# Cached-page work of the decode samples issued two tile-steps earlier in a hybrid S5/MLA step

## The reference, cut to what matters

```python
def mla_sample_attn(q_abs, q_pe, c_new, kpe_new, c_pool, kpe_pool, page_table, w_uv):
    c_past = c_pool[page_table].reshape(dbs, -1, KV_LORA)        # 8 x 2048 x 512
    kpe_past = kpe_pool[page_table].reshape(dbs, -1, QK_ROPE)    # 8 x 2048 x 64
    s_past = (einsum('bqhr,bkr->bhqk', q_abs, c_past) + einsum('bqhe,bke->bhqk', q_pe, kpe_past)) * SOFTMAX_SCALE
    w = softmax(concatenate([s_past, s_new], -1))
    o_lat = einsum('bhqk,bkr->bqhr', w[..., :n_past], c_past) + einsum('bhqk,bkr->bqhr', w[..., n_past:], c_new)
    return einsum('bqhr,rhv->bqhv', o_lat, w_uv)

def mla_prompt_attn(...):   # 8 heads, causal, 528 keys
    o = softmax(where(kpos <= qpos, scores, -inf)) @ c, then w_uv
```

## Time and profile before

| what | us |
|---|---|
| median of 3 runs | 1088.49 (1087.4 to 1095.65) |
| the profiled execution's own time | 1086.38 |
| its span | 1084.5 |
| V stage ends (first `scores` of head 0) | 682.85 |
| attention loop and tail, to the output projection's first product | 682.85 to 874.11 |

### The profile page before, as it was taken

How to read it: one execution, slowest core, us unless ns; L and a number is a source line. 1 busy time by engine, 2 the same in 40 slices (tenths; PEclk the granted TensorE clock), 3 DMA queues, 4 the chain that set the end, 5 groups by cost and what they waited for, 6 DMA issues and landing times.

```text
span 1084.5 us, 26976 instructions
## 1 busy us (share of the span) xinstructions
PE 1026.1 (95%) x10657; PEld 942.7 (87%) x10657; DVE 626.0 (58%) x1341; ACT 381.1 (35%) x805; POOL 157.5 (15%) x257
## 2 busy tenths in 40 slices
PE   5999999999999999999999999788988899999996
PEld 5999999999999999989899987565655569999996
DVE  4685445542676656587785545687888542322333
ACT  6621122222233221145642331544554323322333
POOL 0002310000320000011422412323343100000000
PEclk9999999999999999999999999799999899999999
DMA  9548743322363434165455766858998685233214
GB/s 261 120 135 146 171 109 98 98 72 77 112 166 108 135 98 116 50 156 181 148 154 152 232 197 206 271 185 269 280 297 267 211 272 169 77 104 89 77 39 158
DMA packets 202061, 169.81 MB, mean 157 GB/s; under 512 B 37579, under 2 KB 166086, under 8 KB 200646
## 3 DMA queue, kind: packets, MB, share of 16 engines
q1 hardware_dynamic: 178854, 119.12, 39.4%
q0 software_dynamic: 11616, 29.06, 9.0%
q10 hardware_dynamic: 11496, 20.32, 5.3%
HBM read 140.84 MB, written 25.26 MB: 153 GB/s over the span
## 4 chain that ended last, share of the span: by engine, by line
PE 81%; DVE 6%; ACT 5%; issue 3%; DMA 3%; SPq 0%; POOL 0%; ACTq 0%; DVEq 0%
PE gemm L2156 14%; PE gemm L2157 14%; PE gemm L2158 14%; PE gemm L2525 5%; PE gemm L2527 5%; PE gemm L2526 5%; PE misc L2429 3%; PE gemm L2444 2%; PE gemm L2474 2%; PE misc L2243 1%; PE misc L2196 1%; PE misc L2233 1%; DMA toep<-kall 1%; PE misc L2408 1%; PE gemm L2332 1%
## 5 line engine op out<-in xcount | busy, mean ns | idle before, releaser
L2156 PE MATMUL gemm<-xh,w_hi 128*128 128x260 f32 (+2 forms) x1056 | 302.0, 286 | 0.1
L2157 PE MATMUL gemm<-xl,w_hi 128*128 128x260 f32 (+2 forms) x1056 | 299.9, 284 | 0.0
L2158 PE MATMUL gemm<-xh,w_lo 128*128 128x260 f32 (+2 forms) x1056 | 299.4, 284 | 0.0
L2156 PEld LDWEIGHTS gemm<-xh,w_hi 128*128 128x128 f32 x1056 | 198.7, 188 | 2.6 <-issue 1.9
L874 ACT ACTIVATE w_hi<-w_raw 128x2048 fp32r<-128x2048 f32 (+3 forms) x63 | 90.7, 1440 | 312.6 <-PE gemm L2158 278.8
L2158 PEld LDWEIGHTS gemm<-xh,w_lo 128*128 128x128 f32 x1056 | 199.1, 189 | 0.0
L2157 PEld LDWEIGHTS gemm<-xl,w_hi 128*128 128x128 f32 x1056 | 199.0, 188 | 0.0
L1336 DVE TENSOR_TENSOR w_lo<-w_raw,w_hi 128x2048 fp32r<-128x2048 f32 (+3 forms) x63 | 110.8, 1759 | 152.1 <-ACT w_hi L874 150.1
L2525 PE MATMUL gemm<-comb_hi,w_hi 128*128 128x260 f32 x448 | 128.5, 287 | 1.2 <-DVE comb_lo L2013 1.1
L2527 PE MATMUL gemm<-comb_hi,w_lo 128*128 128x260 f32 x448 | 126.7, 283 | 0.0
L2526 PE MATMUL gemm<-comb_lo,w_hi 128*128 128x260 f32 x448 | 126.6, 283 | 0.0
(11 more groups left out here) (416 smaller groups left out, 2058.2 us busy)
## 6 DMA issues: line engine op xcount, KB each, us to landing
w_raw<-w_in SPq DMA_DIRECT2D x35, 1024.0 KB, 6.3
ckv<-cache_ckv POOLq DMA_DIRECT2D x76, 256.0 KB, 3.9
w_raw<-w_out SPq DMA_DIRECT2D x16, 1024.0 KB, 5.8
ckv<-cache_ckv SPq DMA_DIRECT2D x52, 256.0 KB, 3.7
z_d<-ev ACTq DMA_DIRECT2D x16, 260.0 KB, 2.0
w_raw<-w_glu SPq DMA_DIRECT2D x8, 512.0 KB, 4.1
yt<-x_prompt SPq DMA_DIRECT2D x4, 1024.0 KB
w_raw<-w_uq SPq DMA_DIRECT2D x8, 384.0 KB, 3.6
```

The lines of the kernel that those rows point to most:

```text
L2156: pe.matmul(acc, a, xa, start=k == 0, stop=False)
L2157: pe.matmul(acc, a, xb, start=False, stop=False)
L2158: last = pe.matmul(acc, b, xa, start=False, stop=k == k_tiles - 1)
```

## The change

`LEAD = 2`: all page work of the samples stands two steps earlier against the prompt's tiles.

- Groups 0 and 1 are turned by VectorE in the V stage (v = 5 and 6) into a buffer of their own, `ct_first`, on dead weight memory; the first pair is scored by TensorE in the V stage at v == 8, ahead of that tile's transposes. To free the scores' bank `gemm[2]` the V tiles take turns on three banks (`V_BANK`). ScalarE's spreading into `rep` moves from v == 6 to v == 5, and `build_query(0)` from behind the stage to v == 6. SP, ScalarE and VectorE each wait once for that first pair (`sc_ready` 1) before memory of `ct_first` is written again.
- In the loop pair p is scored in step 2p - 1 instead of 2p + 1, and group n + 3 is turned in step n.
- Sample s has its maximum and exponential in step 4s + 2; VectorE's `turn_sample_weights` stands ahead of that step's page transposes. Its weights are spread at the top of step 4s + 3, ahead of that step's `scores`, and copied by ScalarE behind that step's `exponential`. Its groups are summed in steps 4s + 4 (two, between `turn_last_weights` and `weigh_values`), 4s + 5 and 4s + 6.
- `copy_o`, `build_query`, the samples' stores and the reloads move along. The last sample's groups are summed two in step 31, one behind `turn_last_weights`, one behind the last `weigh_values`.
- Slots 3, 4 and 5 of the ring change places, SP loads group 5 instead of 3, and `cnew` has another address.

```diff
-            return 4 * (i // 4) + 4 + ((0, 2, 3, 4) if i // 4 < N_SAMPLE - 2 else (0, 2, 2, 2))[i % 4]
+            return min(4 * (i // 4) + 4 - LEAD + ((2, 2, 3, 4) if i // 4 < N_SAMPLE - 1 else (1, 1, 2, 2))[i % 4], N_TILES)
...
-        BY_SYNC = 3
+        BY_SYNC, LEAD = 5, 2
...
@@ SP
+            sp.wait_ge(sc_ready, 1)
             for h in range(2):
                 load_v(h)
...
@@ ScalarE, loop
                 scale_rows(n)
-                if n % 4 == 0 and n >= 8:
-                    copy_o(n // 4 - 2)
+                s = (n + LEAD) // 4 - 1 if (n + LEAD) % 4 == 0 else -1
                 if n % 4 == 0 and n:
                     copy_last_turned(n - 1)
-                    sample_exp(n // 4 - 1)
+                if s >= 0:
+                    sample_exp(s)
                 if n + 1 < N_TILES:
                     exponential(n + 1)
-                if n % 4 == 0 and n:
-                    sample_weights(n // 4 - 1)
-                    if n // 4 + 1 < N_HEADS:
-                        head_hi(n // 4 + 1)
+                if s >= 1:
+                    copy_o(s - 1)
+                if n % 4 == 0 and n and n // 4 + 1 < N_HEADS:
+                    head_hi(n // 4 + 1)
+                if n % 4 == 3:
+                    sample_weights(n // 4)
                 copy_turned(n)
...
@@ VectorE, V stage
+                if v in (5, 6):
+                    turn_pages(v - 5, 0, 2)
+                    turn_pages(v - 5, 2, 4)
+                    turn_rotary(v - 5)
...
@@ VectorE, loop
-                if n % 4 == 0 and n:
-                    sample_max(n // 4 - 1)
+                group = n + 1 + LEAD
+                if (n + LEAD) % 4 == 0:
+                    sample_max((n + LEAD) // 4 - 1)
...
                     maximum(n + 1)
-                    turn_pages(n + 1, 0, 2)
-                if n % 4 == 0 and n:
-                    turn_sample_weights(n // 4 - 1)
+                if (n + LEAD) % 4 == 0:
+                    turn_sample_weights((n + LEAD) // 4 - 1)
+                if group < N_GROUPS_OF_PAGES:
+                    turn_pages(group, 0, 2)
                 if n + 1 < N_TILES:
                     normalise(n + 1)
-                    turn_pages(n + 1, 2, 4)
-                    turn_rotary(n + 1)
+                if group < N_GROUPS_OF_PAGES:
+                    turn_pages(group, 2, 4)
+                    turn_rotary(group)
...
@@ TensorE, V stage
+                    if v == 8:
+                        page_scores(0, 0, 16)
...
@@ TensorE, loop
             for n in range(N_TILES):
+                if n % 4 == 3:
+                    spread_page_weights(n // 4)
                 if n + 1 < N_TILES:
                     scores(n + 1)
+                if n % 4 == 0 and n:
+                    turn_last_weights(n - 1)
                 for i in range(N_GROUPS_OF_PAGES - 4):
-                    if freed_at(i) == n and i % 4:
+                    if freed_at(i) == n:
                         weigh_pages(i // 4, i % 4)
                 if n % 4 == 0 and n:
-                    turn_last_weights(n - 1)
                     weigh_values(n // 4 - 1)
-                    spread_page_weights(n // 4 - 1)
-                if n % 2:
-                    page_scores(n // 2, 0, 6)
+                pair = (n + LEAD) // 2 if n % 2 else N_PAIRS
+                if pair < N_PAIRS:
+                    page_scores(pair, 0, 6)
                 turn_weights(n)
-                for i in range(0, N_GROUPS_OF_PAGES - 4, 4):
-                    if freed_at(i) == n:
-                        weigh_pages(i // 4, 0)
+                if n == N_TILES - 1:
+                    for c in range(2):
+                        weigh_pages(N_SAMPLE - 1, c)
...
             turn_last_weights(N_TILES - 1)
+            weigh_pages(N_SAMPLE - 1, 2)
             weigh_values(N_HEADS - 1)
-            spread_page_weights(N_SAMPLE - 1)
-            for c in range(4):
-                weigh_pages(N_SAMPLE - 1, c)
+            weigh_pages(N_SAMPLE - 1, 3)
```

More of the change, by code:

```diff
@@ L1081, in head_hi, with build_query @@
                 act.activation(hh[h % 2][:], hraw[:], ACT.Copy).then_inc(head_hi_done, 1)
+            def build_query(s):
+                if s >= 2:
+                    act.wait_ge(sc_ready, 2 * s - 2)
+                for a in range(4):
+                    rows, cols = slice(32 * a, 32 * a + 32), slice(a * N_HEADS, (a + 1) * N_HEADS)
+                    act.activation(qx[rows, s % 2, :, cols], rep[rows, 0:16, :, s], ACT.Copy)
+                    last = act.activation(qxr[rows, s % 2, :, cols], rep[rows, 16:18, :, s], ACT.Copy)
+                last.then_inc(query_built, 1)
             for v in range(10):
@@ L1794, in head_lo, with turn_pages, turn_rotary @@
                 tt(hh[u][low, rot_cols], hraw[low, rot_cols], hh[u][low, rot_cols].bitcast(F32), ALU.subtract).then_inc(head_lo_done, 1)
+            def turn_pages(n, first, last):
+                by_sync = (1 if first == 0 else 0) if n >= RING else (1 if n == BY_SYNC else 0)
+                dve.wait_ge(page_loaded[by_sync][n % RING], loaded_counts(n)[by_sync])
+                if first == 0 and n >= 3:
+                    dve.wait_ge(sc_ready, (n - 3) // 2 + 1)
+                out = ct_first[:, n, first:last] if n < 2 else ct[:, n % 3, first:last]
+                dve.transpose(out=out.rearrange("p x r -> p (x r)"),
+                              in_=ckv[n % RING][:, first:last].rearrange("p x r -> p (x r)"))
+            def turn_rotary(n):
+                dve.transpose(out=kt[:, n % 3].rearrange("p x e -> p (x e)"), in_=kpe[n % RING][:].rearrange("p x e -> p (x e)")
+                              ).then_inc(page_turned, 1)
             dve.wait_ge(rope_loaded, 64)
@@ L1903, in _ @@
             maximum(0)
+            dve.wait_ge(sc_ready, 1)
             dve.wait_ge(c_t_ready, 6)
@@ L2347, in scores, with page_scores @@
                 last.then_inc(scores_ready, 1)
+            def page_scores(pair, first, last):
+                s, half = divmod(pair, 2)
+                if first == 0:
+                    pe.wait_ge(page_turned, 2 * pair + 2)
+                if first == 0 and half == 0:
+                    pe.wait_ge(query_built, s + 1)
+                    if s >= 2:
+                        pe.wait_ge(sexp_done, s - 1)
+                buffers = buffers_of(pair)
+                c0 = (s % 2) * P + half * 64
+                for r in range(first, last):
+                    for j in range(4):
+                        pe.matmul(SC[32 * j:32 * j + 32, c0:c0 + 64].rearrange("p (g t) -> p g t", g=2), qx[:, s % 2, r, :],
+                                  turned(pair)[:, buffers, j, r * 32:(r + 1) * 32], start=r == 0, stop=False)
+                if last < 16:
+                    return
+                for e in range(2):
+                    for j in range(4):
+                        last = pe.matmul(SC[32 * j:32 * j + 32, c0:c0 + 64].rearrange("p (g t) -> p g t", g=2), qxr[:, s % 2, e, :],
+                                         kt[:, buffers, j, e * 32:(e + 1) * 32], start=False, stop=e == 1)
+                last.then_inc(sc_ready, 1)
             pe.wait_ge(gemm_read, B_V + 2)
@@ L2430, in weigh_values @@
                 last.then_inc(pv_done, 1)
-            def page_scores(pair, first, last):
-                s, half = divmod(pair, 2)
-                if first == 0:
-                    pe.wait_ge(page_turned, 2 * pair + 2)
-                if first == 0 and half == 0:
-                    pe.wait_ge(query_built, s + 1)
-                    if s >= 2:
-                        pe.wait_ge(sexp_done, s - 1)
-                buffers = buffers_of(pair)
-                c0 = (s % 2) * P + half * 64
-                for r in range(first, last):
-                    for j in range(4):
-                        pe.matmul(SC[32 * j:32 * j + 32, c0:c0 + 64].rearrange("p (g t) -> p g t", g=2), qx[:, s % 2, r, :],
-                                  ct[:, buffers, j, r * 32:(r + 1) * 32], start=r == 0, stop=False)
-                if last < 16:
-                    return
-                for e in range(2):
-                    for j in range(4):
-                        last = pe.matmul(SC[32 * j:32 * j + 32, c0:c0 + 64].rearrange("p (g t) -> p g t", g=2), qxr[:, s % 2, e, :],
-                                         kt[:, buffers, j, e * 32:(e + 1) * 32], start=False, stop=e == 1)
-                last.then_inc(sc_ready, 1)
             def spread_page_weights(s):
```

86 lines of the change are left out of this document (32 added, 54 removed).

## The result

The changed kernel takes 1099.24 us (median of 7 runs, 1095.45 to 1104.62), the kernel before 1090.61 us in the same comparison: a ratio of 1.0105, 95% interval 1.0073 to 1.0137. The forecast was 1087, no change; the result is slower by about 1%, inside the range and outside the likeliest case. The profiled execution took 1099.02 us, its span is 1097.3 us, 12.8 more than that of the profiled execution before.

A forecast was written before the change was run, and what follows sets the result against it. A closed chain of waits between TensorE and VectorE, 20.2 us a head, was taken as the bound. 0 + 1.2 + 3.9 - 3.4 - 2.7 = -1.0 gave 1085.4, forecast 1087 by the median, range 1071 to 1104.

The forecast's parts named there:

- the term of the six heads: Steps 4 to 27: 0.65 us more a head, with the old order's stalls kept at their sum; +3.9 us.
- late pages: Rival: pages of group 4s + 8 land 1 us late a head, 1094 us; chance 0.10, shared with unchanged `head_hi`.
- The clean head: A head of the attention loop without stalls: -1.36 + 0.3 + 1.73 = +0.67, to 20.85 us.
- (a): Spreading moves to step 4s + 3, so `head_hi` follows `exponential` and `head_lo` no longer waits: -1.36 us a head.
- (b): Two sums ahead of the weighted values hide TensorE's 0.71 us round trip but add 1.04: +0.3 us a head.
- The gate waits: VectorE, behind its pages of a head's first step, waits 1.5 us or more at the gate in each head.
- (c): Sample's maximum moves to a head's third step, into VectorE's chain, with the weights' transpose: +1.73 us, bounds 0 and 1.73.
- The clock rival: Rival: 2.1 us of TensorE idling in step 4s + 3 drops its clock; 2.7 us a head, 1106; chance 0.20.
- V stage and head 0: Up to step 4: the first pair's 2.4 us hidden, 0; head 0's new sample maximum less some slack, +1.2.
- step 0's wait for ScalarE: At head 0, step 0 waits 3.79 us for ScalarE, so TensorE's scores coming 2.4 us later cost 0.
- Step 28 and the tail: Last head's first step 12.26 to 8.9 us, -3.4; tail to the output projection 26.96 to 24.3 us, -2.7.

The follow-up runs named there:

- the even version: Changed kernel with a sample's first group summed in step 4s + 3 instead of in 4s + 4 beside the second: 1087.34 us, ratio 1.0001.
- the filled version without reloads: Changed kernel without the page ring's reloads, with 14 dummy products in TensorE's three gaps of step 4s + 3: 1089.61 us, ratio 1.0013.

## Why the prediction was wrong

**The step that failed** is the cost at nothing of the reloads in the term of the six heads: +3.9 us were forecast and +15.5 measured. Without reloads the two orders differ by 7.2 there; the reloads add 12.8 to the changed order and 4.6 to the old one. The prediction priced late pages only as a rival, with 1 us a head and a chance of 0.10, at the group whose slot is freed first (4s + 8). That group came in time; the third one did not, by up to 5.5 us. The working counted one slot's issue and landing at the landing times of the earlier trace rows, which were those of an evenly fed queue. It did not ask what the DMA engines do meanwhile. In five heads of the changed kernel, 715 to 835 us, the two largest queues move 30.6 MB, 6.1 a head; at the 297 GB/s that the even version reaches in its stretch without idling that is an estimate of some 20.6 us, a whole head, which leaves no room to make up for idle time of these engines. The change makes them idle 3 to 4 us a head: the samples' pages are wanted two steps earlier, but the first sum of a sample, which frees a slot, stays in step 4s + 4, now beside the second. The head is then the transfer plus the idling, 23.6 to 24.6 us by these numbers; 23.41 was measured, and by the packets 3.6 of it are idle and 19.8 are not. The Trainium skill ("Trainium Kernel Development and Optimization", "Key Constraints") has all queues on the same 16 engines; the runs agree so far as GpSimd's pages land in 3.1 us and not 4.9 when SyncE's are not loaded.

That this is the cause is shown by the even sums, with all the bytes and one sum a step earlier: 1087.3 us, 11 to 12 less. Without reloads and with half of them the changed order takes 1086.3 to 1086.6. That all three lie at the forecast of 1087 is luck. The forecast kept the old order's stalls, and without reloads, where these are gone, the change still costs 10.8 us and not -1: the first pair on TensorE, two falls of the clock, a stall and a longer clean head. With even sums that loss is balanced by the old order's 11 us of stalls, of which the changed order keeps less (3.0 us of issue stalls, 7.2 before).

**The clean head** was forecast at 20.85 and is 20.49, but not by the steps of the prediction. (a) The wait for `head_hi` was worth 0.1 and not 1.36: VectorE's chain closed no sooner than TensorE's own work, 18.5 us and its gaps. The prediction took one closed chain for the bound where a second lay 0.1 us behind it; its joint at 791.07 was a coincidence, as the earlier trace rows show no idle time of TensorE ahead of those page scores. (b) The round trip is worth its 0.71, by the run with it hidden. The gate waits came as forecast (1.56 us in a clean head without reloads, 1.5 or more forecast). (c) TensorE's order has three gaps in step 4s + 3, of 0.66, 0.46 and 0.96 us: 18.41 + 2.08 = 20.49. They wait for what follows the sample's maximum on VectorE; that the maximum makes them is argued, for with it moved out of step 4s + 2 the gaps only moved.

**The clock rival** came true as a mechanism without deciding the result. Without reloads the falls stand in two of six heads and go when the gaps are filled; in the changed kernel they stand in five, with even sums in two, so most of them came with the late pages. The Trainium skill ("TensorE: Matmul & The Clock Gate", "A second HAM failure mode: psum-queue depth-cycling") expects such swings from short idling between groups of products; the run without reloads agrees in two heads, while four with the same gaps keep 1.00. The rival was priced at 2.7 us a head and costs 1.5 where it happens without reloads, and what was held against it, the clean head's 0.71 and 0.34, are smaller gaps.

**V stage and head 0:** forecast 0 and +1.2. From the V stage's eighth tile to step 4 are 33.96 us before and 37.55 after, +3.6; in the pair without reloads +2.2, which is the first pair's time on TensorE (forecast 2.4). The claim that step 0's wait for ScalarE hides it was wrong.

**Step 28 and the tail:** step 28 is gap-free as its parts said (6.12 against 6.6), and `turn_weights(31)` waits for ScalarE 3.47 us (forecast 3.4). (The tail's two bounds add up to 21.6 and 26.3, not 21.7 and 26.4, which changes nothing.) But these were gains on stalls of one old execution: without reloads both orders take 30.9 us from step 28's scores to the output projection, the changed one 1.8 less in step 28 and 1.8 more behind it. The old step 28 was long by its reloads, with an issue stall of 1.64 us and weighted values of 4.96 us. So the -6.1 and -2.3 belong to the stalls, which the changed order has elsewhere, and that -2.3 is near the forecast -2.7 is luck.

What stays open: how the old order's 11 us divide. Bytes are a part (half of them give back 6 us), and most of the issue stalls go with the traffic; what ends these stalls is in the last section.

## What to carry to other kernels

Where the bytes of a period take the DMA engines nearly the whole period, their idle time can become time of the stage, as in the changed order here: before moving work ahead in a ring of buffers, list for each slot the step that frees it and the step that wants it, and keep the freeing even; here one sum of four, one step earlier, is worth 11 to 12 us. In the old order, with fewer bytes in the same steps, the same bunching cost nothing. A wait on an engine is worth only what lies between it and the next closed chain, so look for the engine whose own work nearly fills the period before pricing a wait at its length.

## What the runs showed that was not expected

Reloads that hardly any instruction waits for cost the old order 11 us, in good part by stalls of TensorE with no releaser in the profile: 7.2 us from 690 to 860 at full reloads, 1.3 with half the bytes, 0.4 with none. The DMA view lists queues of instructions beside those of data (in the changed kernel, 715 to 835 us):

```profile
q8 instruction: 17, 0.28, 1.0%
q14 instruction: 10, 0.08, 0.2%
```

The stalls end with q8. In the 16 traces, 690 to 860 us, TensorE has 63 issue stalls of over 0.2 us beside the round trips, and every one ends 1.2 to 1.6 us after a packet of q8 has landed; of TensorE's other instructions one in twenty starts in such a time. The 1.71 us ahead of 819.91, for one, end 1.37 us after a packet that landed at 818.54. The plain reading is that TensorE stands there until its next instructions have come. That full DMA engines make these packets late is argued from 7.2, 1.3 and 0.4; no run varied it alone, and one stall of 2.44 us stands in the filled version without reloads.

Page waits of 18.5 us in nine places cost nothing in the old order, where each was at most 3.2 us, and in the changed order 24.0 us in eight, the longest of 5.5, stand beside a loss of 12.
